# Gated channel mixer: the gate product and its split into a high and a low part, as one instruction of 1024 columns in place of two of 512

## What is computed

```python
def conv_ffn(h, w_up, conv_w, conv_b, w_down):
    u = h @ w_up                      # 2048 -> 2 * 5632
    up = jnp.pad(u, ((0, 0), (CONV_WIDTH - 1, 0), (0, 0)))
    y = conv_b
    for i in range(CONV_WIDTH):       # three causal taps per channel
        y = y + up[:, i:i + S] * conv_w[i]
    a, g = jnp.split(y, 2, axis=-1)
    return (jax.nn.silu(g) * a) @ w_down
```

## Time and profile before

| | us |
|---|---|
| median of 3 runs | 2158.59 |
| lowest and highest | 2158.58, 2162.47 |
| the profiled execution | 2159.26 |
| its span, first to last instruction | 2157.6 |

### The profile page before, as it was taken

One profiled execution on the slowest core, in us unless ns is written; L12 is line 12 of the kernel. 1 busy time (PEld: TensorE's weight loads), 2 busy tenths in 40 slices (PEclk: granted clock), 3 DMA queues, 4 the chain that ended last, 5 costly groups with the idle time before them and its releaser, 6 DMA issues.

```text
span 2157.6 us, 38202 instructions
## 1 busy us (share of the span) xinstructions
PE 2058.2 (95%) x13842; PEld 1901.3 (88%) x13842; DVE 1628.0 (75%) x2261; ACT 1014.6 (47%) x1353; POOL 304.8 (14%) x459
## 2 busy tenths in 40 slices
PE   3889999999999999999999999899999999999998
PEld 3668998987999979999789988799988999889996
DVE  5767888888878798887897786887865566655665
ACT  3117564453555534445444454555543445434453
POOL 3332222224211121111221110011100000000000
PEclk8989999999999999999999999999999999999999
DMA  9989998987777799777897775377755555555552
GB/s 333 360 321 317 360 334 301 353 305 282 247 262 252 272 349 334 258 280 277 292 352 267 282 278 173 111 265 281 254 175 195 176 194 175 195 194 177 186 184 98
DMA packets 235521, 555.69 MB, mean 258 GB/s; under 512 B 13992, under 2 KB 15000, under 8 KB 235160
## 3 DMA queue, kind: packets, MB, share of 16 engines
q1 hardware_dynamic: 180120, 352.93, 47.8%
q0 software_dynamic: 55296, 201.35, 25.7%
HBM read 552.14 MB, written 2.10 MB: 257 GB/s over the span
## 4 chain that ended last, share of the span: by engine, by line
PE 75%; DVE 9%; DMA 8%; issue 4%; ACT 3%; POOL 0%; DVEq 0%; ACTq 0%; POOLq 0%
PE ps L511 17%; PE ps L513 17%; PE ps L512 17%; PE ps L536 7%; DMA mraw<-in_w_mod 7%; PE ps L538 6%; PE ps L537 6%; DVE macc L1211 3%; DVE w_lo L1197 3%; ACT work L883 1%; DMA pmat<-in_w_mod 1%; PE ps L574 1%; ACT w_hi L883 1%; PE ps L556 1%; ACT macc L883 1%
## 5 line engine op out<-in xcount | busy, mean ns | idle before, releaser
L1197 DVE TENSOR_TENSOR w_lo<-raw,w_hi 128x1024 fp32r<-128x1024 f32 x640 | 771.2, 1223 | 384.6 <-ACT w_hi L883 383.1
L883 ACT ACTIVATE w_hi<-raw 128x1024 fp32r<-128x1024 f32 x640 | 668.4, 1056 | 794.0 <-PE ps L513 509.6
L511 PE MATMUL ps<-h_hi,w_hi 128*128 128x256 f32 x3200 | 911.1, 285 | 5.6 <-DVE w_lo L1197 3.9
L513 PE MATMUL ps<-h_hi,w_lo 128*128 128x256 f32 x3200 | 907.3, 284 | 0.0
L512 PE MATMUL ps<-h_lo,w_hi 128*128 128x256 f32 x3200 | 907.2, 284 | 0.0
L511 PEld LDWEIGHTS ps<-h_hi,w_hi 128*128 128x128 f32 x3200 | 616.1, 193 | 7.2 <-issue 6.1
L512 PEld LDWEIGHTS ps<-h_lo,w_hi 128*128 128x128 f32 x3200 | 616.2, 193 | 0.1
L513 PEld LDWEIGHTS ps<-h_hi,w_lo 128*128 128x128 f32 x3200 | 615.9, 192 | 0.0
L1211 DVE SCALAR_TENSOR_TENSOR macc<-mraw,cond,macc 128x512 f32<-128x512 f32 x636 | 438.7, 747 | 61.6 <-DMA mraw<-in_w_mod 55.7
L419 POOL DMA_DIRECT2D mraw<-in_w_mod x366 | 265.4, 725 | 1238.6 <-DVE macc L1211 752.6
L536 PE MATMUL ps<-w_hi,g_hi 128*128 128x512 f32 x832 | 329.6, 396 | 14.1 <-DVE w_lo L1197 14.0
(11 more groups left out here) (144 smaller groups left out, 1126.8 us busy)
## 6 DMA issues: line engine op xcount, KB each, us to landing
mraw<-in_w_mod POOLq DMA_DIRECT2D x366, 512.0 KB, 6.2
raw<-in_w_up SPq DMA_DIRECT2D x176, 1024.0 KB, 5.1
raw<-in_w_down SPq DMA_DIRECT2D x88, 1024.0 KB, 5.2
raw<-in_w_attn_in SPq DMA_DIRECT2D x48, 1024.0 KB, 8.1
raw<-in_w_attn_out SPq DMA_DIRECT2D x16, 1024.0 KB, 7.7
work<-in_w_mod POOLq DMA_DIRECT2D x12, 512.0 KB, 8.8
raw<-in_w_pool SPq DMA_DIRECT2D x4, 1024.0 KB, 5.3
pmat<-in_w_mod POOLq DMA_DIRECT2D x6, 512.0 KB, 11.0
```

The costliest lines, as they stand in the source:

```text
L511: mm(o, wh, ah, start=st, stop=False, skip_group_check=True)
L513: i = mm(o, wl, ah, start=False, stop=last_half and kk == 1, skip_group_check=True)
L883: return nc.scalar.activation(o, i, f, **kw)
L1197: V.tensor_tensor(w_lo[:, s, :, :], raw[:, j % 4, h * 1024:(h + 1) * 1024].rearrange("p (k n) -> p k n", k=2), w_hi[:, s, :, :].bitcast(F3 ...
```

## The change

At the end of a pair the product, the copy and the subtraction are each one instruction over all four tiles (1024 columns) in place of two over two tiles (512 columns). The two silus stay as they are. The one product waits for both, the one copy for the whole product, the one subtraction for the whole copy. Each increments its semaphore by two, so the counts that others wait for are unchanged.

```diff
@@ ACT, up_pair @@
                         for b in range(2):
                             act.wait_ge((bank0_free, bank1_free)[b], g + 2 * i + 2)
                             A(yg[:, 2 * b:2 * b + 2, :], yg[:, 2 * b:2 * b + 2, :], ACT.Silu).then_inc(silu_done, 1)
-                        for b in range(2):
-                            act.wait_ge(gg_ready, 2 * i + (2 * (gi + g0) + b + 2))
-                            A(g_hi[:, ds(4 * i + 2 * b, 2), :], yg[:, 2 * b:2 * b + 2, :],
-                              ACT.Copy).then_inc(ghi_ready, 1)
+                        act.wait_ge(gg_ready, 2 * i + (2 * (gi + g0) + 3))
+                        A(g_hi[:, ds(4 * i, 4), :], yg[:, :, :], ACT.Copy).then_inc(ghi_ready, 2)
@@ DVE, up_pair @@
-                        for b in range(2):
-                            dve.wait_ge(silu_done, 2 * i + (2 * (gi + g0) + b + 1))
-                            dve.wait_ge((bank0_free, bank1_free)[b], g + 2 * i + 1)
-                            V.tensor_tensor(yg[:, 2 * b:2 * b + 2, :], yg[:, 2 * b:2 * b + 2, :],
-                                            ya[:, 2 * b:2 * b + 2, :], ALU.mult).then_inc(gg_ready, 1)
-                        for b in range(2):
-                            dve.wait_ge(ghi_ready, 2 * i + (2 * (gi + g0) + b + 1))
-                            V.tensor_tensor(g_lo[:, ds(4 * i + 2 * b, 2), :], yg[:, 2 * b:2 * b + 2, :],
-                                            g_hi[:, ds(4 * i + 2 * b, 2), :].bitcast(F32),
-                                            ALU.subtract).then_inc(glo_ready, 1)
+                        dve.wait_ge(silu_done, 2 * i + (2 * (gi + g0) + 2))
+                        dve.wait_ge(bank1_free, g + 2 * i + 1)
+                        V.tensor_tensor(yg[:, :, :], yg[:, :, :], ya[:, :, :], ALU.mult).then_inc(gg_ready, 2)
+                        dve.wait_ge(ghi_ready, 2 * i + (2 * (gi + g0) + 2))
+                        V.tensor_tensor(g_lo[:, ds(4 * i, 4), :], yg[:, :, :],
+                                        g_hi[:, ds(4 * i, 4), :].bitcast(F32),
+                                        ALU.subtract).then_inc(glo_ready, 2)
```

## The result

Over 12 executions each the changed kernel takes 2165.48 us in the median (2160.79 to 2170.10) and the kernel before 2159.36 (2155.19 to 2165.25). The ratio is 1.0029 with a 95% interval of 1.0020 to 1.0039, which on 2159.4 is +6.3 us, 4.3 to 8.4. The forecast was +5.05, slower. The profiled execution took 2167.45 with a span of 2165.8. That is 8 us longer than the profiled execution of before, more than the kernels differ by, and 2.3 of it had arisen before the first channel mixer began. So what follows reads waits and distances inside the mixers, not spans.

A forecast was written before the change was run, and what follows sets the result against it. PE, 95% busy, was taken as the bound, so only delays it waits for count: 1.3 + 1.3 + 0.93 + 0.59 + 0.93 = 5.05 us on the median 2158.59 gives 2163.6, range 2160.5 to 2167.5.

The forecast's parts named there:

- Lost overlap: End of each pair: DVE and ACT no longer overlap on halves; ACT is 0.93 us later, DVE 1.17.
- rival 1: All 22 pairs: engines' time counts, not the chain; DVE saves 0.32 per pair, 7.0 us less, 2151.6; chance 0.03.
- The five block ends: Pairs ending blocks at 742, 1028, 1268 (layer 0), 1858, 2084 (layer 1): PE sees the delay, 5.05 us in sum.
- five tight pairs: Ordinary pairs, layer 1's second and third block: `w_lo` hidden with 0.03 to spare, taken at 0, at most 0.2 each.
- 1582: Block end in layer 1 where PE also fills the gate's rows and does not wait for `w_lo`; taken at 0.
- The first term of the chain: Ordinary pair at 1720: one product waits for the second silu, starts at 1721.23 like today's second product, ends 1722.45.
- ends with a table load: Block ends at 1268 (layer 0) and 2084 (layer 1): ACT's delay reaches PE in full, +0.93 us each.
- the end at 1858: Block end in layer 1: `w_lo` may start at 1862.59 but comes at 1863.18, a new PE wait of +0.59 us.
- ends with a transfer: Block ends at 742 and 1028 (layer 0): `w_mod` pieces, loads and PE's wait all move with DVE, +1.3 us each.
- the clock behind 758 and 1045: Layer 0, stretches behind the two long PE waits: forecast keeps the clock as before, chance 0.5; wrong if it behaves otherwise.
- Rival 2: Layer 0's two long waits: clock (0.65 each) or transfer gives part back, no measurable change, 2162.3; chance 0.3.
- Rival 3: PE's waits growing to 1.97 (1275) and 1.63 (2090): one drops the clock, 2.85 us on top, 2166.5; chance 0.12.

The follow-up runs named there:

- second profiles: Kernel before and changed kernel each profiled once more, nothing changed; PE waits 4.68 and 5.99 us behind the first transfer.
- the halves: Kernel before with its 512-column instructions kept, but product, copy and subtraction each waiting for the whole as in the change; ratio 1.0042, +9.1 us.
- the 2.89: Kernel before, 512-column instructions, next splits moved ahead; at two layer 0 block ends copies behind ACT's first products, subtractions behind first three pieces; ratio 0.9964, -7.8 us.

## Why the prediction was right, and where it was not

**The mechanism.** Lost overlap, as forecast. Taking the whole waits with the old instructions costs 9.1 us, taking the new instructions behind the splits costs nothing that can be measured (0.9991 beside 0.9990 in halves). The fixed cost saved is real: of the 9 us that DVE is less busy, the products and subtractions make 6.7, near the 7.0 of rival 1. It bought nothing, since where PE waits it is the order of the steps that sets the next `w_lo`, and DVE stands idle between them. Rival 1 falls with that. The Trainium skill's rule on large tiles (VectorE: DVE Perf Modes, "The TRN2 errata — SBUF-src ops pay a fixed extra latency per instruction") goes the way of rival 1; the runs agree with it on the price of an instruction (1.23 for one of 1024 columns, 1.38 for two of 512), not on the time.

**The places.** The five block ends, each by name, and none else but the five tight pairs. 1582 has no wait, as taken.

**The sizes.** The first term of the chain was mis-sized: "the one product must wait for the second silu, which is when the second product starts today: 1721.23". Today the second product starts 0.04 behind the end of the silu, on a DVE that is still busy with the first. In the changed kernel, the product at the last block end, then silu and table load on ACT:

```profile
2091.93 1.23 DVE L1468 TENSOR_TENSOR work<-work 128x1024 f32<-128x1024 f32 x1 [0.86 <-ACT work L883]
...
2091.11 0.63 ACT L883 ACTIVATE work<-work 128x512 f32<-128x512 f32 x1 [0.93 <-DVE work L1437]
...
2094.37 1.28 ACT L883 ACT_TABLE_LOAD   x1
```

silu ends at 2091.74, the product starts at 2091.93: 0.19, on a DVE that stands idle. The 0.15 more goes into every delay. At the second block end the chain shows what lies in it, from the silu's end at 1032.66 to the product at 1032.84:

```profile
1032.69 0.04 DVEq L1467
```

L1467 is the second of the two waits that stand ahead of the product, and DVE's sequencer goes through it only when silu is done. In the kernel before the chain has 0.02 between the second silu and the second product, while DVE was at the first. That the waits make the 0.15 is read from the chain, not tested by a run.

| | forecast | measured |
|---|---|---|
| ends with a table load | 0.93 each | 1.10 each |
| the end at 1858 | 0.59 | 0.60 listed as a wait, 0.84 from mark to mark |
| five tight pairs | 0, "0.03 in hand" | 0.15 each, 0.75 in all |
| ends with a transfer, as waits | 1.3 each | 1.34 and 1.32; second profiles 1.31 and 0.11 |
| the same, from mark to mark | 1.3 each | 0.97 and 0.70; second profiles 1.00 and -0.32 |

The tight pairs are a case that the prediction named as one that would show it wrong: a margin of 0.03 read from a trace is no margin. A second case that it named is the clock behind 758 and 1045, which is next. The sum of what was measured in the first pair of profiles is 2.20 + 0.84 + 0.75 + 2.66 = 6.45.

**The clock.** Rival 2 was right in part. Behind the two long waits the clock is at its lower level again, the windows that follow PE's start:

```profile
762.40:767.00 4.60, 4.56 (x11) 3.62 (x12) 4.57 (x7) 0.00 (x0) 1.12 (x3) 0.50 0.89 303
...
1049.90:1053.70 3.80, 3.76 (x9) 3.01 (x10) 3.77 (x6) 0.00 (x0) 0.85 (x2) 0.50 0.84 271
```

4.6 us at 0.50 and 3.8, where the kernel before had 5.7 and 5.9 (its window from 1045.3 to 1051.2). PE resumes later and the clock does not rise as much later, so half of the difference comes back, 0.55 and 1.05. From mark to mark the two stretches are 0.97 and 0.70 longer, 0.37 and 0.62 less than their waits grew, which this more than covers. How much comes back differs between executions, too: in the second profile of the kernel before the clock is low for 4.9 us behind a wait of 4.68, where it was 5.7 behind 4.62. The changed kernel has 4.2 and 4.0 in its second profile. So the direction is shown, and the size only to about half a microsecond. By the terms the channel mixers of this profile are 6.45 - 0.99 = 5.46 us longer; by the marks and the last end it is 4.72 + 1.10 = 5.82, the rest lying between layer 0's table load and the first mark of layer 1's mixer, where 1.45 are lost and not 1.10 (in that stretch, between 1330 and 1350, the clock also falls in 7 of the 13 profiles of all runs, whatever the kernel). The forecast of 5.05 was near partly by luck: two terms of opposite sign were left out of it, the 0.15 of each handing over and the clock's share.

Rival 3 was right in part, too: waits near 2 us drop the clock in some executions. It stays up behind 2.14 and 1.80 in the first profile of the changed kernel, but falls behind 1.81 in the second (0.51 for 3.4 us), behind 1.94 in the second profile of the kernel before (0.52), behind 2.33 and 1.90 in the halves. The 13 profiles of all runs have 21 waits of PE for `w_lo` between 1.6 and 2.4 us, and the clock falls behind 7 of them; it falls behind none of the shorter ones and behind all 26 of the long ones, 2.89 and up. Each fall behind a wait near 2 us costs half of 3.4 us, 1.7. By growing 1.04 to 2.14 and 0.70 to 1.80 the change makes two more such places. An estimate from these counts is 2 x 7/21 x 1.7 = 1.1 us in the mean; the profile of 5.8 had none of it, and with it the sum is 6.9, within the 4.3 to 8.4 of the ratio, as is the sum without it.

**The transfer.** The chain has these transfers in the first profile of the changed kernel, at the first and the second block end, and this one in the kernel before at the second:

```profile
754.48 5.24 DMA mraw<-in_w_mod
...
1040.96 6.26 DMA mraw<-in_w_mod
...
1036.21 6.38 DMA mraw<-in_w_mod
```

5.24 and 6.26 us, where the kernel before had 5.30 and 6.38. So in this pair of profiles the waits compare at nearly equal transfers. The transfers start later by what DVE is late: at the first end 14.28 behind ACT's mark for 12.84, in both pairs of profiles, at the second 13.54 for 12.05. PE's wait follows at 742 (4.62 and 4.68 against 5.96 and 5.99) and, the other way round, in the 2.89. Behind 1028 the prediction's "All of it moves with DVE" does not always hold: in the second profile of the kernel before the last transfer that PE waited for was one released by ACT, 7.60 us long, and the difference to the changed kernel was 0.11 and not 1.32. What this end costs in the mean stays open.

## What to carry to other kernels

Where two engines hand halves to each other, joining the halves takes the overlap away, and the chain grows by about the length of what ran in parallel, whatever fixed cost is saved (here 1.36 us up to the next `w_lo` at the tight pair, for 0.3 us of DVE's time). Count the distance from the last input to the next thing that others wait for, not busy time. Before joining instructions look at what stands behind them in their lists: here moving the next splits ahead of the end of the pair removed waits that joining had made longer. Behind the moved splits the form made no difference that could be measured in one pair of runs, and a difference of 4 us by the ratios, 1.35 by the profiles, in the other, where the product still stood ahead of the long waits. A margin shorter than one handing over between engines, 0.1 to 0.2 us here, is better taken as gone.

## What was not expected of the hardware

- The product on DVE started 0.02 to 0.04 behind the end of ACT's silu when DVE was just finishing another instruction (1721.19 to 1721.23), and 0.18 to 0.19 behind it when DVE had stood idle (2091.74 to 2091.93; idle 0.86 ahead of it).
- Behind waits of PE of 1.6 to 2.4 us the granted clock fell to its 1.2 GHz level in 7 of 21 cases: it stayed at 1.00 behind 1.94 and read 0.52 behind the same 1.94 in the second profile of the same kernel.
- The transfers of `w_mod` that PE's long waits hung on took 5.24 to 5.35 us at the first block end and 6.05 to 6.38 at the second in the profiles of the two kernels, but 6.56 at the first and 5.70 at the second in the run with the splits moved ahead and the new instructions, and the one released by ACT 7.60.
- A loss of 0.15 us where PE starts a half unit, and one of 0.33 per pair in the halves with whole waits, shows in no view of waits, since the matmul ahead is still listed as running.
